# State space scan in four chains at once, two of its products on GpSimd, and its norm tile by tile

## The reference

```
CHUNK = 128; SSD_HEADS = 32; SSD_HEAD_DIM = 64; SSD_GROUPS = 8; D_STATE = 128
per direction, head h and chunk of 128 rows (dta = dt * -exp(a_log), decays are sums of dta):
  rows(l)  = sum over s up to l of (C_l . B_s) * exp(sum of dta over s+1..l) * dt_s * x_s     inside the chunk
           + exp(sum of dta up to l) * (C_l . state)                                          from the state
  state    = exp(sum of dta over the chunk) * state
           + sum over s of B_s * exp(sum of dta after s) * dt_s * x_s
y = rows of both directions + d_skip * x
y = rmsnorm over groups of 256 of (y * silu(z)) * g ;  h = h + gate * (y @ w_out)
```

## Time and profile before

| | before |
|---|---|
| median of 3 runs (lowest to highest) | 3715.18 us (3706.55 to 3715.83) |
| the profiled execution, its span | 3716.41 us, 3714.7 us |
| PE busy, share of the span | 3310.6 us, 89% |
| DVE busy | 2041.5 us, 55% |
| ACT busy | 1497.9 us, 40% |
| POOL busy | 227.5 us, 6% |
| mean granted TensorE clock | 0.935 |

### The profile page before, as it was taken

One profiled execution on the slowest core, in us unless ns is written; L12 is line 12 of the kernel. 1 busy time (PEld: TensorE's weight loads), 2 busy tenths in 40 slices (PEclk: granted clock), 3 DMA queues, 4 the chain that ended last, 5 costly groups with the idle time before them and its releaser, 6 DMA issues.

```text
span 3714.7 us, 54191 instructions
## 1 busy us (share of the span) xinstructions
PE 3310.6 (89%) x22580; PEld 2835.0 (76%) x22580; DVE 2041.5 (55%) x2686; ACT 1497.9 (40%) x2090; POOL 227.5 (6%) x267
## 2 busy tenths in 40 slices
PE   7989999898998999989798689887999899775897
PEld 6978887797887788788586578885888678664695
DVE  4556645556555664555524666754333466666554
ACT  5445454445454544454522433323222344201443
POOL 1000000000000000000001133320000000000000
PEclk9989999899998999999899789988999899877899
DMA  7755545575774555467440000003332134200454
GB/s 221 227 155 175 153 151 181 160 228 185 210 225 146 158 173 152 159 193 225 139 127 22 1 8 3 2 2 93 96 92 98 54 99 111 74 1 12 134 178 136
DMA packets 461611, 460.79 MB, mean 124 GB/s; under 512 B 18272, under 2 KB 347152, under 8 KB 461264
## 3 DMA queue, kind: packets, MB, share of 16 engines
q1 hardware_dynamic: 454720, 435.42, 39.3%
q0 software_dynamic: 6672, 22.23, 1.9%
HBM read 456.54 MB, written 1.05 MB: 123 GB/s over the span
## 4 chain that ended last, share of the span: by engine, by line
PE 75%; DVE 16%; ACT 5%; issue 3%; DMA 1%; POOL 0%; DVEq 0%; ACTq 0%; SPq 0%; POOLq 0%
PE banks L304 20%; PE banks L306 19%; PE banks L305 19%; DVE weights_lo L290 1%; PE banks L1874 1%; PE banks L1873 1%; PE banks L3485 1%; PE banks L4208 1%; PE banks L1299 1%; PE banks L3487 1%; PE banks L3466 1%; DVE arena L3885 1%; PE banks L4259 1%; PE banks L1896 1%; PE banks L4238 1%
## 5 line engine op out<-in xcount | busy, mean ns | idle before, releaser
L290 DVE TENSOR_TENSOR weights_lo<-raw_weights,weights_hi 128x1024 fp32r<-128x1024 f32 (+1 forms) x463 | 548.7, 1191 | 505.7 <-ACT weights_hi L282 430.6
L282 ACT ACTIVATE weights_hi<-raw_weights 128x1024 fp32r<-128x1024 f32 (+1 forms) x463 | 473.9, 1031 | 629.0 <-PE banks L306 626.3
L255 DVE TENSOR_TENSOR weights_lo<-raw_weights,weights_hi 128x1024 fp32r<-128x1024 f32 x180 | 220.8, 1228 | 476.7 <-ACT weights_hi L248 288.3
L248 ACT ACTIVATE weights_hi<-raw_weights 128x1024 fp32r<-128x1024 f32 x180 | 190.4, 1059 | 520.8 <-PE banks L306 513.8
L304 PE MATMUL banks<-first_input_split,weights_hi 128*128 128x256 f32 x1320 | 380.2, 288 | 13.7 <-DVE weights_lo L290 6.8
L306 PE MATMUL banks<-first_input_split,weights_lo 128*128 128x256 f32 x1320 | 375.9, 285 | 0.0
L305 PE MATMUL banks<-first_input_split,weights_hi 128*128 128x256 f32 x1320 | 374.1, 283 | 0.0
L290 DVE TENSOR_TENSOR third_weights_split<-raw_weights,third_weights_split 128x1024 fp32r<-128x1024 f32 (+1 forms) x205 | 246.1, 1200 | 165.4 <-ACT third_weights_split L282 130.3
L282 ACT ACTIVATE third_weights_split<-raw_weights 128x1024 fp32r<-128x1024 f32 (+1 forms) x205 | 212.1, 1035 | 209.7 <-PE banks L306 208.2
L304 PE MATMUL banks<-work_split,weights_hi 128*128 128x512 f32 (+2 forms) x776 | 271.6, 350 | 22.2 <-DVEq L2372 18.4
L305 PE MATMUL banks<-input_split,weights_hi 128*128 128x512 f32 (+2 forms) x776 | 270.1, 348 | 0.0
(11 more groups left out here) (599 smaller groups left out, 7140.0 us busy)
## 6 DMA issues: line engine op xcount, KB each, us to landing
raw_weights<-in_w_ffn_gu SPq DMA_DIRECT2D x176, 512.0 KB, 4.9
raw_weights<-in_w_in SPq DMA_DIRECT2D x144, 512.0 KB, 3.6
raw_weights<-in_mlp_w SPq DMA_DIRECT2D x128, 512.0 KB, 3.9
raw_weights<-in_ada_w SPq DMA_DIRECT2D x96, 512.0 KB, 4.3
raw_weights<-in_w_ffn_down SPq DMA_DIRECT2D x80, 512.0 KB, 3.4
raw_weights<-in_w_branch SPq DMA_DIRECT2D x48, 512.0 KB, 3.6
raw_weights<-in_ssd_w_in SPq DMA_DIRECT2D x48, 512.0 KB, 3.9
raw_weights<-in_w_mkv SPq DMA_DIRECT2D x32, 512.0 KB, 3.9
```

Source lines behind the costliest of these rows:

```text
L248: last = s.activation(self.w_hi[:, u % 2, :], self.raw[:, u, :], ACT.Copy)
L255: last = v.tensor_tensor(self.w_lo[:, u % 2, :], self.raw[:, u, :], self.w_hi[:, u % 2, :].bitcast(F32), ALU.subtract)
L282: last = s.activation(hi, raw, ACT.Copy)
L290: last = v.tensor_tensor(lo, raw, hi.bitcast(F32), ALU.subtract)
```

## The change

- `Scan` takes the place of `Half`: four chains, one for each direction and half of the heads, all begun together. Each has two PSUM banks in place of four, its own `xdt`, `state`, `seg_l` and `seg_e`, and its C.B lies in the context half of `b_t`. Their steps are written in turn, one of each chain (`in_turn`). The join between the directions goes. A chain that comes to a main tile second waits for the first one's rows.
- `seg_l` is made on POOL, and so is `xdt` on main tiles. The second spread of a tile is queued on POOL behind the first eight heads' L4208 step (now L4215).
- On context tiles dt is scaled first (128x16), then xs times that: one 128x1024 product in place of two. On main tiles `xdt` is scaled in place; on the last tile not at all. The first tile of a chain makes only the sum that the state needs, the last only the one that the rows need. Rows are added to y by 8 heads (128x512) twice, in place of 16 once.
- The norm goes tile by tile: DVE times z; ACT squares with the sum accumulated (8 of 128x256); root; reciprocal; DVE times it; 16 transposes; the weights are a column per feature, applied on the copy out of PSUM, 8 blocks by ACT and 8 by DVE.
- The gate's diagonals, spread and copy stand behind the ends of all chains and ahead of the squares on ACT's queue. The weights' broadcast load goes; a load of the column stands ahead, with the layer's other parameters.

```diff
-    class Half:
+    class Scan:
-        def __init__(self, q):
-            self.q, self.chain = q, c.chains[q]
+        def __init__(self, d, q):
+            n = 2 * d + q
+            self.chain, self.pooled, self.pools = c.scans[n], c.decays_spread[n], 0
+            self.first_bank, self.q, self.other, self.first_rows = 2 * n, q, None, None
...
+        def spread(part):
+            done = ch.steps
+            @ch.block.gpsimd
+            def _(p):
+                p.wait_ge(ch.steps_done, done)
+                heads = slice(g.heads.start + 8 * part, g.heads.start + 8 * part + 8)
+                p.tensor_tensor(g.seg_l, g.after.unsqueeze(1).broadcast_to([P, 8, P]),
+                                g.dta[:, tile, heads].unsqueeze(2).broadcast_to([P, 8, P]),
+                                ALU.mult).then_inc(g.pooled, 1)
...
+        if main:
+            spread_made = spread(0)
+            @ch.block.gpsimd
+            def _(p):
+                p.wait_ge(ch.steps_done, start)
+                p.tensor_tensor(g.xdt, as_heads(xs[:, tile, g.columns]), over_width(g.dt[:, tile, g.heads]),
+                                ALU.mult).then_inc(g.pooled, 1)
...
+                @ch.block.tensor
+                def _(pe):
+                    pe.wait_ge(g.pooled, made)
+                    pe.wait_ge(ch.steps_done, ch.steps)
+                    for h in range(8):
+                        last = pe.matmul(g.bank(h // 4)[:, h % 4 * P:(h % 4 + 1) * P], g.seg_l[:, h, :], g.incl,
+                                         start=True, stop=True)
+                    last.then_inc(ch.steps_done, 1)
+                ch.steps += 1
+                if part == 0:
+                    spread_made = spread(1)
...
-    for d, order in enumerate(((2, 3, 0, 1), (3, 2, 1, 0))):
-        c.begin_chains()
...
-        c.end_chains()
-
-    gate = Gate(c, 1, 2, 1, cols(c.par, 0, 1, D))
-    gate.spread(0, [])
...
-    gain = cols(c.par, 1024, D_IN)
-    c.load(gain, a["ssd_norm_g_2"][0, :].partition_broadcast(P))
-    c.loaded()
+    scans = [Scan(d, q) for d in range(2) for q in range(2)]
...
+    in_turn([scan(g) for g in scans[:2]], [scan(g) for g in scans[2:]], 0)
...
+    gate = Gate(c, 1, 2, 1, cols(c.par, 1024, 1, D))
+    gate.spread(4, ends)
+    try_root(c)
...
+            for n in range(SSD_G):
+                last = s.activation(squares_of[t][:, n, :], y_g[:, n, :], ACT.Square, scale=1.0 / 16,
+                                    accum_out=ss[:, t, n:n + 1])
...
+            for k in range(SSD_G):
+                last = s.activation(y_t[:, k, t * P:(t + 1) * P], turned(k), ACT.Copy, scale=parts.gain[:, k:k + 1])
...
+            for k in range(SSD_G, 2 * SSD_G):
+                last = v.tensor_scalar(y_t[:, k, t * P:(t + 1) * P], turned(k), parts.gain[:, k:k + 1], None, ALU.mult)
```

More of the change, by code:

```diff
@@ L4105, in __init__ @@
-            self.off = ([cols(c.par, 1024, half_heads, SSD_P), cols(w, 6144, half_heads, SSD_P)])[q]
-        def bank(self, n):
[L4108 to L4117, removed]
+            self.dt, self.dta = inputs.dt[:, d], inputs.dta[:, d]
@@ L4121, in _ @@
                 pe.wait_ge(ch.steps_done, ch.steps)
[L4123 to L4125 removed]
+                for n in range(half_groups):
+                    last = pe.matmul(g.bank(n // 2)[:, n % 2 * SEQ:(n % 2 + 1) * SEQ],
+                                     c_t[:, g.q * half_groups + n, tokens],
+                                     g.state[:, n * 4:(n + 1) * 4, :].rearrange("p h d -> p (h d)"), start=True, stop=True)
                 last.then_inc(ch.steps_done, 1)
+            ch.steps += 1
+            yield
             @ch.block.vector
@@ L4129, in _ @@
                 v.wait_ge(ch.steps_done, ch.steps)
[L4130 to L4140, removed]
-            ch.steps += 1
-        for g in halves:
-            ch = g.chain
+                v.tensor_tensor(g.off, g.two_banks(SSD_P), over_width(g.ex[:, 1, :]), ALU.mult).then_inc(ch.steps_done, 1)
@@ new lines, in chunk, with _ @@
+            ch.steps += 1
+            while last_chunk and g.other.first_rows is None:
+                yield
+            y_g = as_heads(y[:, tile, g.columns])
+            @ch.block.vector
+            def _(v):
+                if last_chunk:
+                    v.wait_ge(g.other.chain.steps_done, g.other.first_rows)
+                v.wait_ge(ch.steps_done, ch.steps)
+                v.tensor_tensor(y_g, y_g, g.off, ALU.add).then_inc(ch.steps_done, 1)
+            ch.steps += 1
+            yield
@@ L4145, in _ @@
+            if last_chunk:
+                return
+            g.first_rows = ch.steps
             @ch.block.vector
@@ L4147, in _ @@
                 v.wait_ge(ch.steps_done, ch.steps)
-                v.tensor_tensor(g.xw, g.xdt, over_width(g.ex[:, 0, :]), ALU.mult).then_inc(ch.steps_done, 1)
+                v.tensor_tensor(g.xdt, g.xdt, over_width(g.ex[:, 0, :]), ALU.mult).then_inc(ch.steps_done, 1)
             ch.steps += 1
[L4150 to L4165, removed]
-                                         start=True, stop=True)
-                    last.then_inc(ch.steps_done, 1)
-                ch.steps += 1
[L4169 to L4227, removed]
@@ new lines, in chunk, with _ @@
+        yield
+        @ch.block.tensor
+        def _(pe):
+            pe.wait_ge(ch.steps_done, ch.steps)
+            for n in range(half_groups):
+                group = g.q * half_groups + n
+                last = pe.matmul(g.bank(n // 2)[:, n % 2 * SEQ:(n % 2 + 1) * SEQ], b_tok[:, tile, group * P:(group + 1) * P],
+                                 g.xdt[:, n * 4:(n + 1) * 4, :].rearrange("p h d -> p (h d)"), start=True, stop=True)
+            last.then_inc(ch.steps_done, 1)
+        if not first:
+            @ch.block.vector
+            def _(v):
+                v.wait_ge(ch.steps_done, ch.steps)
+                v.tensor_tensor(g.state, g.state, over_width(g.ex[:, 2, :]), ALU.mult).then_inc(ch.steps_done, 1)
@@ new lines, in chunk, with _, scan @@
+        ch.steps += 1 if first else 2
+        yield
+        @ch.block.vector
+        def _(v):
+            v.wait_ge(ch.steps_done, ch.steps)
+            if first:
+                v.tensor_copy(g.state, g.two_banks(SSD_P)).then_inc(ch.steps_done, 1)
+            else:
+                v.tensor_tensor(g.state, g.state, g.two_banks(SSD_P), ALU.add).then_inc(ch.steps_done, 1)
+        ch.steps += 1
+        yield
+    def scan(g):
+        for n, tile in enumerate(g.order):
+            yield from chunk(g, tile, n == 0, n == NT + 1)
@@ new lines, in in_turn, with _ @@
+    def in_turn(running, late, ticks):
+        at = 0
+        while running or late:
+            if late and at == ticks:
+                running, late = running + late, []
+            at += 1
+            running = [x for x in running if next(x, True) is None]
+    scans = [Scan(d, q) for d in range(2) for q in range(2)]
+    for g, other in zip(scans, scans[2:] + scans[:2]):
+        g.other = other
+    begun = c.steps
+    @c.block.gpsimd
+    def _(p):
+        p.wait_ge(c.steps_done, begun)
```

265 lines of the change are left out of this document (156 added, 109 removed).

## The result

| | before | after |
|---|---|---|
| median of all runs (lowest to highest) | 3712.98 us (3706.55 to 3715.83, 4 runs) | 3656.42 us (3648.04 to 3660.06, 4 runs) |
| the profiled execution | 3716.41 us | 3655.16 us |
| ratio of times, 95% interval | | 0.9842 (0.9830 to 0.9854) |

What follows compares the result with a forecast made beforehand. The scan was taken as a latency chain alternating between PE and DVE, with PE the bound under four chains. Scan 133 us for 197.2 (64 less) and norm 6 less took 3716.4 to 3646 us, range 3627 to 3670.

Steps and rivals of the forecast that it cites:

- rival 2: Scan: clock stays at 0.82 because PE still has gaps; 134 us of PE, 13 waiting, time 3660; chance 0.13.
- The context tiles: Scan's first stretch: 22 us at full clock, with slower products and 2 us of round ends 28 us, for 39 before.
- The first main tile: Middle main tile of four chains: PE 50.2 us, some 4 idle, 2 for late adds to y; 56.5 us.
- The last: Last main tile of four chains: PE 41 us, lateness 3, last add 0.7; 44.6 us.
- the sum above keeps PE as the bound with about 5 us of lateness: Main tiles: DVE's 37 us and POOL's 49 exclude each other at the port, 86 us in 101, so PE still bounds.
- The walk without its cold starts: Scan stepped through chain by chain: context tiles 28, middle main tile 56.5 and last main tile 44.6 us.
- Cold starts: Main tiles: PE runs at half clock for a while after gaps; two starts and a partial one, 4 us.
- Rival 1: Main tiles: POOL and the port bind, with POOL products at 2.9 us; scan 148, time 3661; chance 0.2.
- Rival 4: Scan: PE at half clock throughout, time 3745; slower than before once PE's work passes some 195 us; chance 0.02.
- DVE's work: Scan: DVE loses 44 us of products and gains a few small ones, from 131.4 to about 90 us.
- The norm: After the scan: squares wait for the gate's copy, tile 1's product for tile 0's copies; 36 us for 42.1.
- The test named in advance: Profile after: wrong if L4215 mostly waits for POOL, clock is under 0.85, or tile 1 isn't behind tile 0's copies.

Runs made afterwards that it cites:

- e1: Changed kernel with DVE's product with C.B reading exponentials from PSUM and the state's part scaled in place in PSUM: 3633.9 us, 0.9785 of before.
- e10: The kernel of e7 run again, beside e9 on the same chip: 3619.5 us, 0.9754 of before.
- e5: e1 with DVE's product with C.B done twice into the same place: 3645.4 us, 11.5 above e1.
- e3: Changed kernel with direction 0's two chains run to their end, a join, then direction 1's two: 3670.3 us, 13.9 above the change.
- e7: Changed kernel with the edits of e1 and e4 together: 3617.6 us, 0.9734 of before.
- e9: The kernel of e8 run again in more rounds, beside e10 on the same chip: 3614.5 us, 0.9736 of before.
- e4: Changed kernel with the norm's gate spread and copy behind the squares, and DVE's tile 1 product ahead of tile 0's copies: 3637.8 us.
- e8: e7 with the state's scaling on the first main tile moved to POOL: 3619.3 us (3606.3 to 3633.5).
- e2: Changed kernel with POOL's spreads and xdt product back on DVE: 3668.9 us, 12.5 above the change.
- e6: Changed kernel with the norm of before grafted on the new scan: 3661.8 us, 5.4 above the change.

## Why the prediction was right, and where it was not

The time fell in the range, but partly by luck. The forecast's own sum was 11.5 us short in the scan, and the mechanism that came true there is that of rival 2, which had a chance of 0.13: PE at a clock of about 0.82 because it still has gaps. Its two terms, 134 us of PE and 13 of waiting, measured 132.9 and 11.6. The range held since it reached to the rivals.

- *What bounds.* Right: with four chains PE is the fuller engine, 132.9 of 144.5 us.
- *The context tiles,* forecast 28 us: 24.9. The allowance for slow products and round ends was too large.
- *The first main tile,* forecast 56.5 and up to 4 for cold starts: 68.1. *The last,* 44.6: 51.5. Here the sum failed, at the step "the sum above keeps PE as the bound with about 5 us of lateness". The port's exclusion was forecast and its waits were about as large (4.3 us more idle time than in e1); what was missing is that such rounds take PE's clock with them (14.9 us more busy time). With the conflict removed (e1) the two are 59.5 and 40.9 us, and the whole scan 125.4, a start of the first main tile at half clock still in it.
- *The walk without its cold starts,* 129 us. The nearest run is e10, with no conflict and the main tiles at a clock of 0.97 and 1.00: 119.0 us. So the walk was 10 us too long: 24.9 us for 28 on the context tiles, 53.1 for 56.5 and 41.0 for 44.6 on the main ones. At the handover PE waited 1.92 us, where the walk had 4, and no L4215 step waited for an add to y. This error hid a part of the clock's cost.
- *Cold starts,* 4 us in the sum: too few. The forecast counted only the ones behind long gaps; in most rounds waits of 0.4 and 0.8 us did it too (e5, the change). The rule cited there, of the Trainium skill, page "TensorE: Matmul & The Clock Gate", section "HAM oscillation — how this bites in real kernels", gave 3651 where I took 3646. This trace agrees with the rule for the three waits over 1 us inside the scan, of 1.72, 2.54 and 1.92 us: 9.62 us for 32 instructions that take 7.17, 2.06 for 8 that take 1.14, and 10.07 for 7.17. The section's own case is longer waits, for a DMA; that waits under 1 us can do it is what the runs here show, and e3 shows that they need not.
- *Rival 1* had its mechanism (2.85 us for a pair at the port), but a POOL product alone stays at 1.90 us in e1, `xdt` too, for which I took 2.3. POOL was busy 54.6 us in the change and 44.7 without conflict.
- *Rival 4's* threshold was a little high: with its 13 us of waiting and the norm 6 us shorter, the change is slower than before once PE's work passes 190 us, not 195.
- *DVE's work,* 90 us: 91.9 in e1, 105.8 in the change with the port's waits in it.
- *The norm,* 36 us: 34.9. The order of events was as forecast: the squares at 10.8 us (forecast 10.5), tile 1's product behind tile 0's copies. Two small terms were off: eight squares took 3.3 us, not 4.4, and a scaled copy 0.27 (2.17 for 8), not 0.34.
- *The test named in advance,* "wrong if clock is under 0.85", was met (0.81), and rightly so: it is the part that was wrong. "L4215 waits for POOL" was not: PE's waits were for DVE.

## What to carry to other kernels

Moving elementwise work to GpSimd won 12.5 us here while VectorE's products beside it had both operands in SBUF, and 35 once they read one from PSUM. So have ScalarE write its result back in place in PSUM instead of to SBUF, which cost nothing here and was worth 22 us. When several chains keep TensorE nearly full, allow for short waits in a row of steps at up to several times their length, because the clock can follow (14.9 us more busy time for 4.3 of waiting here, 8.9 for 2.8 in e5). And after cutting a stage by tiles, read each queue once more in order: a small step of another task (here a gate's copy, 1 us long, which itself waits for POOL and PE) ahead of the critical one delayed it by 8.

## What was not expected of the hardware

- Waits of 0.42 us before three of four PE steps of 1.97 us are followed by half clock (5.33 us for 32 instructions that take 3.73 at full clock), and so are most rows of waits of 0.8 us, but not all (e3: 3.79 us behind four of them). In e1, with one wait of 1.92 us and none other over 0.3 in 80 us, the clock is 0.98.
- The first main tile began at half clock in some executions and at full clock in others, with the same program ahead of it. From the first sum to the first L4183 step it took 36.9 us in the change, e1, e7 and e9 (36.8), and 31.3 in e4, e5, e8 and e10; e2 (half) and e6 (full) show the same two kinds. PE's wait ahead of that tile was 2.5 us in the first kind and 1.0 in the second. The second kind had a slower second context step instead (8.7 us for 7.17). This is 5.6 us of the scatter of 12 us and more between runs of one kernel; what decides it stays open.
- A spread and a product at the port together take 2.85 us, less than their 1.90 and 1.22 alone (3.12). In a row without conflict each starts 1.86 and 1.14 us behind the one before, which is 3.00: the exclusion is not quite complete, or start and end overlap more.
